# Adding the log of the key gate into the decay exponents of a gated linear recurrence, in place of products on GpSimd and VectorE

## The reference, cut to what matters

```
logf = log_sigmoid(zf) + log1p(lb * exp(-zf))
k    = (1 - lb) * sigmoid(-zf)
b    = cumsum(logf)                         # within a block
attn[t,s] = sum_d q[t,d] * k[s,d] * exp(b[t,d] - b[s,d])      # s <= t
o    = attn @ v + (q * exp(b)) @ S
S    = exp(b_last) * S + (k * exp(b_last - b))^T @ v
```

## Time and profile before

| what | value |
|---|---|
| device time, three executions | 869.84, 870.59, 870.81 us |
| median | 870.59 us |
| profiled execution, span from its first to its last instruction | 868.0 us |
| granted TensorE clock, mean | 0.992 of full speed |
| busy in the span: TensorE, VectorE, ScalarE, GpSimd | 826.0, 412.5, 238.2, 80.0 us |

### The profile page before, as it was taken

How to read it: one execution, slowest core, us unless ns; L and a number is a source line. 1 busy time by engine, 2 the same in 40 slices (tenths; PEclk the granted TensorE clock), 3 DMA queues, 4 the chain that set the end, 5 groups by cost and what they waited for, 6 DMA issues and landing times.

```text
span 868.0 us, 12770 instructions
## 1 busy us (share of the span) xinstructions
PE 826.0 (95%) x4976; PEld 536.6 (62%) x4976; DVE 412.5 (48%) x691; ACT 238.2 (27%) x377; POOL 80.0 (9%) x141
## 2 busy tenths in 40 slices
PE   4999999999999999999999999999999999999993
PEld 2989899989999867586353453543535335353351
DVE  6788889988999963876010302103021030210235
ACT  6666655665456415111101010000100001000011
POOL 1344455430000000000000000000000000000000
PEclk9999999999999999999999999999999999999997
DMA  8222222254343712499899999999999999999981
GB/s 317 74 83 84 82 82 82 106 181 148 145 146 123 318 45 103 185 400 413 327 429 430 426 429 427 427 428 427 427 428 430 428 427 430 425 431 424 430 362 62
DMA packets 32006, 251.07 MB, mean 289 GB/s; under 512 B 4638, under 2 KB 8094, under 8 KB 19674
## 3 DMA queue, kind: packets, MB, share of 16 engines
q1 hardware_dynamic: 29424, 249.17, 70.3%
q10 hardware_dynamic: 2538, 1.32, 0.5%
HBM read 247.99 MB, written 2.48 MB: 289 GB/s over the span
## 4 chain that ended last, share of the span: by engine, by line
PE 59%; DVE 21%; ACT 9%; DMA 8%; issue 2%; ACTq 1%; DVEq 0%
PE ps L507 58%; DVE ar L1730 5%; DMA ring<-in_w_down_end 4%; DMA ring<-in_w_gate_e 4%; DVE ring L1608 4%; DVE split_t L1737 3%; ACT ring L1157 2%; ACT ar L1167 1%; DVE ar L1644 1%; ACT split_w L1076 1%; DVE ar L1655 1%; DVE ar L1599 1%; PE ps L881 1%; ACTq L1206 1%; ACT ar L1129 1%
## 5 line engine op out<-in xcount | busy, mean ns | idle before, releaser
L507 PE MATMUL ps<-ring,ar 128*64 128x512 f32 (+1 forms) x1088 | 226.8, 568 | 4.3 <-ACT ar L1361 3.3
L507 PEld LDWEIGHTS ps<-ring,ar 128*64 128x64 f32 x1088 | 88.5, 137 | 130.3 <-issue 120.6
L507 PE MATMUL ps<-ring,xT 128*64 128x512 f32 (+2 forms) x896 | 161.1, 458 | 2.8 <-DMA ring<-in_w_gate_e 2.8
L507 PEld LDWEIGHTS ps<-ring,xT 128*64 128x64 f32 (+1 forms) x896 | 85.9, 152 | 72.8 <-issue 67.1
L2019 DVE TENSOR_TENSOR ar<-ar,ps 128x512 f32<-128x512 f32 (+1 forms) x42 | 28.8, 685 | 214.6 <-PE ps L507 214.5
L507 PE MATMUL ps<-split_x,split_t 128*128 128x320 f32 x672 | 101.0, 310 | 0.5 <-DVE split_t L1737 0.5
L507 PEld LDWEIGHTS ps<-split_x,split_t 128*128 128x128 f32 x672 | 98.6, 188 | 2.5 <-issue 1.4
L507 PE MATMUL ps<-split_x,split_w 128*128 128x320 f32 x480 | 79.4, 321 | 5.6 <-ACT ar L1212 1.7
L507 PE MATMUL ps<-ar 128*128 128x128 f32 (+7 forms) x340 | 80.1, 382 | 0.1
L507 PEld LDWEIGHTS ps<-split_x,split_w 128*128 128x128 f32 x480 | 72.8, 192 | 10.3 <-ACT split_x L1111 2.1
L1730 DVE SCALAR_TENSOR_TENSOR ar<-ar,params 128x350 f32<-128x350 f32 x116 | 67.7, 583 | 4.1
(11 more groups left out here) (220 smaller groups left out, 744.7 us busy)
## 6 DMA issues: line engine op xcount, KB each, us to landing
ring<-in_w_gate_e SPq DMA_DIRECT2D x32, 2048.0 KB, 16.5
ring<-in_w_up_e SPq DMA_DIRECT2D x32, 2048.0 KB, 17.3
ring<-in_w_down_e SPq DMA_DIRECT2D x26, 2048.0 KB, 19.7
ring<-in_w_in SPq DMA_DIRECT2D x56, 512.0 KB, 4.1
ring<-in_w_down_end SPq DMA_DIRECT2D x3, 2048.0 KB, 35.3
ring<-in_w_o_a SPq DMA_DIRECT2D x8, 512.0 KB, 5.7
ring<-in_w_out SPq DMA_DIRECT2D x1, 4096.0 KB, 14.7
ar<-in_w_down_e SPq DMA_DIRECT2D x6, 512.0 KB, 17.5
```

What stands on the lines that cost most here:

```text
L507: return pe.matmul(out, lhsT, rhs, start=start, stop=stop)
```

## The change: what it does

VectorE makes one more tile at the end of `forget_in`: hnc = (log of the key without its factor + ln(1 - lb)) - b, that is ln k - b. GpSimd's `key_decay` then writes b at the cut plus hnc in place of b at the cut minus b, so ScalarE's one exponential over X gives decay times key at once. The same tile feeds the three exponentials into hkde. GpSimd's seven products of `key_side` and VectorE's product L1635 are left out. The key itself is still made, for the last level. The log of the key moves from hk to a tile of its own (hlk). Four waits change: TensorE's `levels` waits for E_ready in place of xk_ready, and `prev_kT` for kde_ready in place of kdec_ready; GpSimd's `key_decay` waits for nc_ready in place of b_ready. VectorE has one new wait (k_ready) in `forget_in`, and ScalarE one (nc_ready) ahead of L1167.

```
 # TensorE, levels / prev_kT
-                pe.wait_ge(h["xk_ready"], n1 + 1)
+                pe.wait_ge(h["E_ready"], n1 + 1)
...
-                pe.wait_ge(h["kdec_ready"], 2 * i + b + 1)
+                pe.wait_ge(h["kde_ready"], 3 * (2 * i + b) + 3)
...
 # ScalarE, start; key_exp; tile_exp
-            step(act.activation(lnolb[:, :], olb[:, :], ACT.Ln))
+            signal(act, act.activation(lnolb[:, :], olb[:, :], ACT.Ln), lnolb_ready, 1)
...
-                signal(act, act.activation(hk[:, b, :], hk[:, b, :], ACT.Exp, bias=lnolb[:, bass.ds(n, 1)]), h["k_ready"], n + 1)
+                signal(act, act.activation(hk[:, b, :], hlk, ACT.Exp, bias=lnolb[:, bass.ds(n, 1)]), h["k_ready"], n + 1)
...
                 cc(act.activation(heb, hb, ACT.Exp))
+                act.wait_ge(h["nc_ready"], n + 1)
                 for t, (t0, c) in enumerate(TILES):
-                    last = act.activation(hkde[:, t0:t0 + c], hb[:, t0:t0 + c], ACT.Exp, scale=-1.0, bias=hb[:, t0 + c - 1:t0 + c])
+                    last = act.activation(hkde[:, t0:t0 + c], hnc[:, t0:t0 + c], ACT.Exp, bias=hb[:, t0 + c - 1:t0 + c])
...
 # GpSimd
-                pool.wait_ge(h["b_ready"], n + 1)
+                pool.wait_ge(h["nc_ready"], n + 1)
...
-                    ins = pool.tensor_tensor(xv, bv[:, :, hs - 1:hs].to_broadcast([P, w // (2 * hs), hs]), bv[:, :, 0:hs], ALU.subtract)
+                    ins = pool.tensor_tensor(xv, bv[:, :, hs - 1:hs].to_broadcast([P, w // (2 * hs), hs]), nv[:, :, 0:hs], ALU.add)
...
-            def key_side(i, b):
-                n = 2 * i + b
-                pool.wait_ge(h["E_ready"], n + 1)
-                pool.wait_ge(h["k_ready"], n + 1)
-                for lv, hs in enumerate(LV):
...
-                    ins = pool.tensor_tensor(xv, xv, kv, ALU.mult)
...
-                signal(pool, ins, h["xk_ready"], n + 1)
...
 # VectorE, forget_in / carry_side
-                signal(dve, dve.tensor_tensor(hk[:, b, :], hls, ps[:, 0, 0:T], ALU.subtract), h["ls_ready"], n + 1)
+                if not (first and b == 0):
+                    dve.wait_ge(h["k_ready"], n)
+                signal(dve, dve.tensor_tensor(hlk, hls, ps[:, 0, 0:T], ALU.subtract), h["ls_ready"], n + 1)
...
                 signal(dve, dve.tensor_tensor_scan(hb, reset, hls, 0.0, ALU.mult, ALU.add), h["b_ready"], n + 1)
+                signal(dve, dve.scalar_tensor_tensor(hnc, hlk, lnolb[:, bass.ds(n, 1)], hb, ALU.add, ALU.subtract), h["nc_ready"], n + 1)
...
-                dve.wait_ge(h["kde_ready"], 3 * n + 3)
-                dve.wait_ge(h["k_ready"], n + 1)
+                dve.wait_ge(h["kde_ready"], 3 * n + 1)
                 cc(dve.tensor_copy(hebl[:, b, :], heb[:, SEQ - 1:T:DEC]))
...
-                signal(dve, dve.tensor_tensor(hkde, hkde, hk[:, b, :], ALU.mult), h["kdec_ready"], n + 1)
```

More of the change, by code:

```diff
@@ L191, in build @@
         sgu = sgu_f.rearrange("p (b n) -> p b n", b=2)
-        (hq, hk, hV, he, hw, hls, hb, heb, hqeb, hkde, hkT, hAM, hAS, hSA, hosq, hrs, hebl, _, hSst, hSo) = carve(
-            0, 2 * T, 2 * T, 384, T, T, T, T, T, T, T, 384, 3 * LW, 384, P, T, T, 4, 892, 2 * P, 2 * P)
+        (hq, hk, hV, he, hw, hls, hb, heb, hqeb, hkde, hkT, hAM, hAS, hSA, hosq, hrs, hebl, hlk, hnc, _, hSst, hSo) = carve(
+            0, 2 * T, 2 * T, 384, T, T, T, T, T, T, T, 384, 3 * LW, 384, P, T, T, 4, T, T, 892 - 2 * T, 2 * P, 2 * P)
         two = lambda v: v.rearrange("p (b n) -> p b n", b=2)
@@ L242, in build @@
         var0, rstd0, x0_mid, x0_ready, x0T_done = (sem(n) for n in ("var0", "rstd0", "x0_mid", "x0_ready", "x0T_done"))
-        params_ready = sem("params_ready")
+        params_ready, lnolb_ready = sem("params_ready"), sem("lnolb_ready")
         wu_in = [sem(f"wu_in{c}") for c in range(CT)]
@@ L253, in build @@
         names = ("f_done q_done v_done ls_ready w_ready k_ready b_ready dr_ready dl_ready E_ready q_sb ac_ready "
-                 "kde_ready xr_ready xk_ready a_done am_ready as_ready qeb_ready kdec_ready kT_done kT_sb s_done sa_sb o_done "
+                 "kde_ready xr_ready nc_ready a_done am_ready as_ready qeb_ready kT_done kT_sb s_done sa_sb o_done "
                  "osq_ready rms_done rstd_ready rstd_exp o_out so_ready so_stored hc_dve hp_dve hc_act hp_act hc_pool hp_pool fold_ready v_sb round")
@@ L1440, in _ @@
             signal(pool, pool.tensor_tensor(piece(wl, 0), sh[:, 0, 0].rearrange("p k n -> p (k n)"), piece(whF, 0), ALU.subtract), wlo_ready, 1)
-            cc = Chain(pool, h["hc_pool"], 12)
+            cc = Chain(pool, h["hc_pool"], 6)
             pc = Chain(pool, h["hp_pool"], 1)
@@ L1451, in key_decay @@
                     xv = X[b][:, XO[lv]:XO[lv] + w].rearrange("p (m s) -> p m s", s=2 * hs)[:, :, 0:hs]
-                    bv = hb[:, 0:w].rearrange("p (m s) -> p m s", s=2 * hs)
-                    ins = pool.tensor_tensor(xv, bv[:, :, hs - 1:hs].to_broadcast([P, w // (2 * hs), hs]), bv[:, :, 0:hs], ALU.subtract)
+                    bv, nv = (v[:, 0:w].rearrange("p (m s) -> p m s", s=2 * hs) for v in (hb, hnc))
+                    ins = pool.tensor_tensor(xv, bv[:, :, hs - 1:hs].to_broadcast([P, w // (2 * hs), hs]), nv[:, :, 0:hs], ALU.add)
                     if lv < 6:
@@ L1456, in key_decay @@
                 signal(pool, ins, h["dl_ready"], n + 1)
-            def key_side(i, b):
-                n = 2 * i + b
-                pool.wait_ge(h["E_ready"], n + 1)
-                pool.wait_ge(h["k_ready"], n + 1)
-                for lv, hs in enumerate(LV):
-                    w = SEQ if lv == 0 else T
-                    xv = X[b][:, XO[lv]:XO[lv] + w].rearrange("p (m s) -> p m s", s=2 * hs)[:, :, 0:hs]
-                    kv = hk[:, b, 0:w].rearrange("p (m s) -> p m s", s=2 * hs)[:, :, 0:hs]
-                    ins = pool.tensor_tensor(xv, xv, kv, ALU.mult)
-                    if lv < 6:
-                        cc(ins)
-                signal(pool, ins, h["xk_ready"], n + 1)
                 cc.end()
@@ L1488, in head_turn @@
                     level_sums(*prev, first_prev)
-                if cur:
-                    key_side(*cur)
             head_turn((0, 0), None)
@@ L1697, in head_turn @@
                     w_low(*nxt, 1)
+            dve.wait_ge(lnolb_ready, 1)
             head_turn((0, 0), (0, 1), None, None, first=True)
```

## The result

The changed kernel takes 878.71 us (median of four executions, 877.8 to 879.05), the kernel before 870.24 us beside it. The ratio is 1.0093, 95% interval 1.0081 to 1.0105: slower by 8.5 us. I had forecast slower by 4.7 and a range up to 877.4, so the direction is right and the size is not. In the profiled execution (877.8 us) the span is 875.9 us, 7.9 above the span before.

A forecast was written before the change was run, and what follows sets the result against it. The prediction took a closed ScalarE-VectorE loop in the head turns as the bound, 20.0 us against TensorE's 19.2. It summed 0.58 + 3.0 + 1.16 = 4.74 us, giving 870.6 + 4.7 = 875.3 us, range 872.8 to 877.4.

The forecast's parts named there:

- The loop: Head turns: ScalarE's `forget`, VectorE's `forget_in` to differences, ScalarE's exponential over X; 20.0 us a loop turn, delay goes over whole.
- The new operation and its waits: VectorE between scan and mask: 0.55 us plus gap and wait, 0.75 a loop turn, 0.58 a written-out turn.
- The relief: VectorE's query products fall from 3.94 to about 2.4 us a turn without GpSimd's products beside them; the loop gains nothing.
- rival B: Head turns: VectorE's total work sets the pace, so the relief gains 1.3 us a turn, time 861.5; chance 0.05.
- TensorE's idle time: Head turns: TensorE idle about 1 us a turn, waiting for ScalarE's L1212 ahead of the query projection.
- Key differences on GpSimd and exponentials on ScalarE: Head turns: shapes and counts kept, cost 0; GpSimd starts 0.55 or more later, as does VectorE's mask.
- Rival C: Differences in the head turns: GpSimd's later start against VectorE adds 0.5 a turn, 3.5 us, time 878.8; chance 0.07.
- turn 1 itself adds nothing: Turn 1: shorter products remove VectorE's lateness, its mask waits for TensorE anyway, 0.58 later from turn 0; nothing more added.

The follow-up runs named there:

- the version with one tile: Changed kernel with GpSimd's differences again b at the cut minus b, both from b's tile; hnc still made and waited for: 874.69 us, ratio 1.0057.
- the version with the other sign: Changed kernel with hnc made as b minus ln k, GpSimd subtracting and ScalarE's three exponentials at scale -1 as before: 878.78 us, ratio 1.0098.
- the version that filled the wait: Changed kernel with two extra 128x320 matmuls on TensorE, result unread, ahead of head 1's forget projection: 878.78 us, ratio 1.0098.

## Why the prediction was wrong, step by step

*The loop* was right. In the loop turns the delay sits between `forget` and the exponential over X and nowhere else, and it goes over whole: TensorE's wait for the square behind turn 7 ends at 188.42 in place of 179.62, 8.8 later, and the span is 7.9 longer. The delay stays at 8.8 until 395 us and is 7.6 from 399 us on (8.0 at the end): the kernel before had a stretch at half clock there (392 to 397 us, 0.66 granted) and the changed one had none. That part of the 7.9 is chance.

*The new operation and its waits* were right: 0.55 and 0.79 a loop turn against 0.75; as a whole 4.6 us in the version with one tile, against 4.74.

*The relief* was right: 2.45 us for the query products, and nothing from it on the loop. The version without the products shows it. The note of the Trainium skill that I cited under rival B (Advanced Engine Details and Errata, VectorE Performance Modes) speaks of VectorE's two-port instructions. No run here tells whether these f32 products are such; that they are slowed beside GpSimd is what the trace shows (577 against 320 ns).

*TensorE's idle time* I had put down to ScalarE's L1212 alone, 1 us a turn. In the changed kernel six waits for it (now L1213) make 2.8 us and six for VectorE's output product (L1659) 4.7, 1.25 us a turn together. That cost nothing, since `forget` starts 0.9 to 2.0 us after TensorE's projections have ended in turns 2 to 7.

*The step that failed* is the one on the key differences: "Key differences on GpSimd and exponentials on ScalarE keep their shapes and counts: 0". They keep shapes and counts, and yet cost 3.1 us, as the version before with only a second tile shows. (In the changed kernel it is 4.0, which may include what the lower clock in turn 1 adds in some executions.) GpSimd's differences take longer, and VectorE's beside them with them: in turn 0 of the changed kernel, where the two run side by side, VectorE's last 0.04 us longer than GpSimd's each time (0.50 beside 0.46, 0.64 beside 0.59). I priced an operation by its shape and left out where its operands lie. The trace before had a pair to see it by. GpSimd's last product, which reads two tiles, takes 0.60, and its last difference, which reads one, 0.45 (109.16, above):

```profile
118.63 0.60 POOL L1467 TENSOR_TENSOR ring<-ring,ar 128x160 f32<-128x160 f32 x1
```

It is right for the finest halves alone: with halves of 32 frames the products take 0.53, the two-tile differences 0.46.

Rival C had the right place and the wrong cause. It asked for a later start of GpSimd against VectorE, which did not happen. That its 878.8 met the measured 878.71 is luck: it put 3.5 us on the differences, which cost 3.1, and had no term for the rest. (The upper bound of 877.4 was said to lie half-way to C; half-way from 875.3 it is 877.05. The measured time is above both.)

*A second miss, smaller,* is in turns 0 and 1. It is the second tile again and, in some executions, the clock. From head 0's `forget` to head 1's I had added 0.58. The version with one tile adds 0.61 and the one with only two tiles 0.41; the changed kernel adds 1.0 where the clock stays up (the version with the other sign) and 2.55 in the execution shown, where its 48 projections ran 1.54 us longer at the lower clock. That turn 1 itself adds nothing held for the new operation (19.99 us with one tile, 19.97 before).

*The sum again.* From turn 0's `forget` to the exponential of turn 7 the changed kernel needs 9.02 us more than the kernel before. The version with one tile needs 4.81, the one with only two tiles 2.61, and the projections 1.54: 8.96. The version with the other sign, without such a stretch there, needs 7.6. In the medians it is 4.6 + 3.1 = 7.7 of 8.5. The 0.8 that is left would fit 1.54 us in every other execution, but the version that filled the wait did not get faster, so this remainder is argued and not shown.

*What stays open* is why a second tile slows GpSimd. The Trainium skill (Advanced Engine Details and Errata, SBUF Cachelines) says that consecutive accesses to the same 16-byte line run at full speed and accesses to a different line each time pay a penalty. The growth with finer halves (0.46 to 0.59 us) agrees in kind. Against it stands that with one tile the coarse halves too read b at the cut and b[s] from places up to 124 bytes apart (halves of 32 frames), and take the same 0.45 us as the finest. No run here tells lines from anything else that comes with a second tile.

## What to carry to other kernels

Follow the chain once around before pricing a change: what is taken off beside it is worth nothing, and each operation put on it costs its full time once a turn. Price an elementwise operation on an engine that slows another, and is slowed by it, by the row that reads as many different tiles, in runs as short, as the new one will, not by its shape alone. And when an order is changed, ask what the moved work is the last input of: here the masks left one loop and closed the next, and the 3.5 us came only when the sums behind them were made shorter too, and then outside the loop turns. Look at where a gain came from even when its size is the one forecast.

## What the runs showed of the hardware that I had not expected

- A GpSimd tensor_tensor of 128x160 f32 takes 0.45 us at every fineness of the halves when both inputs come from one tile. With two it takes 0.46, 0.47 and 0.48 in halves of 32, 16 and 8 frames, 0.52 in halves of 4 and 0.59 to 0.60 in halves of 2 and 1, whether the tiles are adjacent or not and whether it adds or subtracts, and the same beside VectorE's masks and beside its differences. The one that falls beside VectorE's fold takes longer either way (0.85 with one tile, 0.92 to 1.14 with two). VectorE's seven differences grow with it (from 3.95 to 4.46 us).
- TensorE's granted clock fell to its lower level (1.2 GHz) for 3.4 us in or behind 9 of 17 waits of 2.1 to 2.4 us between the start of the head turns and the reduction behind the last, over all the profiled executions, and at no other place there. In the other 8 it stayed at the upper level (2.4 GHz), at the same places too. Stretches of 3.4 us also came in the later stages without such a wait (393 us in the kernel before), not the same in every execution.
- On VectorE a pointer scalar costs 0.06 us (0.55 against 0.49 for a scalar_tensor_tensor of 128x320). In a hardware loop a further semaphore wait ahead of an operation costs some 0.08 (gaps of 0.12 and 0.20; 0.34 with one more and an address from a register). Written out, these gaps are 0.03 to 0.04.
